# One fused two-block kernel: the context keys and values of the second block are computed at other places, gate products come in halves, and the expert rounds overlap

## The reference

```
first block:
  h = rmsnorm(x);  z = h @ w_in
  o_hg = gated recurrence over q, f_fw, f_bw, i (4 heads of 128, two directions), normed, gated
  o_mla = softmax attention, 8 heads of 96, keys and values from small latents
  merged = sigmoid(gate_a) * (o_hg @ w_oA) + sigmoid(gate_b) * (o_mla @ w_oB)
  x = x + merged @ w_out
  experts: hm = rmsnorm(x); top-1 of 8 groups, then top-2 of its 8 experts
           x += sum of weight * (silu(hm @ w1[e]) * (hm @ w3[e])) @ w2[e]
  x = x + (p @ w_ple_proj) * sigmoid(rmsnorm(x) @ w_ple_gate)
second block:
  hc = rmsnorm(ctx) * (1 + sc_c) + sh_c           # 256 context tokens
  k_c, v_c = split(hc @ w_in_2[:, K_OFF:V_END])   # two matrices of 1024 x 1024
  h = rmsnorm(x) * (1 + sc) + sh;  ten products h @ w_in_2[...]
  conv branch; 16-head neighbourhood attention over x's keys and k_c, v_c
  x = x + gt * rmsnorm(merged @ w_o)
```

## Time and profile before

| | us |
|---|---|
| median of 3 runs (1339.63 to 1343.4) | 1343.25 |
| the profiled execution | 1342.57 |
| its span, from first to last instruction | 1340.4 |
| TensorE busy in it | 1237.3 (92%) |
| VectorE, ScalarE, GpSimd busy | 302.1, 207.4, 107.1 |
| mean granted clock of TensorE | 0.959 of 2.4 GHz |
| moved by DMA | 324.57 MB |

### The profile page before, as it was taken

The page is one execution under the profiler, slowest core; times in us unless marked ns, Lnnn a source line. Parts: engine busy times, 40 slices in busy tenths (PEclk is TensorE's granted clock), DMA queues, the critical chain, the costliest instruction groups (busy, mean ns, idle before and its releaser), DMA issues.

```text
span 1340.4 us, 14669 instructions
## 1 busy us (share of the span) xinstructions
PE 1237.3 (92%) x6021; PEld 858.2 (64%) x6021; DVE 302.1 (23%) x652; ACT 207.4 (15%) x419; POOL 107.1 (8%) x117
## 2 busy tenths in 40 slices
PE   4999899999999989898989889889999999999997
PEld 4887788887853434434343324378888888876686
DVE  2035213543130111101110111121001004426511
ACT  1222452220110000000000000110000000025501
POOL 0015002510100000000000000000000000025300
PEclk9999899999989898898979898998999999999999
DMA  8879323333649999999999999952444444344300
GB/s 286 265 249 321 123 97 123 125 127 102 252 188 401 376 418 409 417 409 419 417 393 418 418 419 413 377 185 94 157 149 147 146 155 157 126 157 124 97 0 32
DMA packets 149737, 324.57 MB, mean 242 GB/s; under 512 B 8655, under 2 KB 111546, under 8 KB 133178
## 3 DMA queue, kind: packets, MB, share of 16 engines
q1 hardware_dynamic: 143818, 315.39, 63.0%
q0 software_dynamic: 1536, 4.20, 1.1%
q10 hardware_dynamic: 4336, 4.30, 1.0%
HBM read 321.77 MB, written 1.05 MB: 241 GB/s over the span
## 4 chain that ended last, share of the span: by engine, by line
PE 77%; DMA 8%; issue 7%; DVE 4%; ACT 2%; SPq 1%; POOL 1%; DVEq 0%; POOLq 0%; ACTq 0%
PE bank L551 31%; PE bank L817 14%; PE bank L554 13%; DMA ring<-in_w 7%; PE bank L837 5%; PE bank L794 3%; DVE X L1732 1%; PE bank L854 1%; PE bank L711 1%; PE bank L909 1%; DMA ring<-in_w_in 1%; PE bank L605 1%; PE bank L942 1%; PE bank L922 1%; ACT AR L1147 1%
## 5 line engine op out<-in xcount | busy, mean ns | idle before, releaser
L551 PE MATMUL bank<-HT,ring 128*128 128x256 f32 x1856 | 409.1, 382 | 4.3 <-DVE HT L1403 3.7
L551 PEld LDWEIGHTS bank<-HT,ring 128*128 128x128 f32 x1856 | 354.8, 192 | 56.4 <-DVE HT L1403 4.4
L817 PE MATMUL bank<-ring,AR 128*64 128x512 f32 x640 | 169.1, 593 | 3.9 <-DMA ring<-in_w 3.9
L554 PE MATMUL bank<-ring,HT 128*128 128x256 f32 (+1 forms) x576 | 129.1, 385 | 8.1 <-DMA ring<-in_w_in 6.9
L817 PEld LDWEIGHTS bank<-ring,AR 128*64 128x64 f32 x640 | 56.4, 137 | 112.9 <-issue 112.9
L554 PEld LDWEIGHTS bank<-ring,HT 128*128 128x128 f32 x576 | 110.3, 196 | 24.6 <-issue 8.2
L817 PE MATMUL bank<-AR 128*64 128x512 f32 x384 | 125.0, 663 | 0.1
L837 PE MATMUL bank<-ring,AR 128*64 128x512 f32 x384 | 87.7, 598 | 11.4 <-ACT AR L1147 11.4
L554 PE MATMUL bank<-ring,AR 128*128 128x256 f32 x328 | 74.5, 390 | 4.4 <-DVE AR L1850 1.5
L1720 DVE TENSOR_TENSOR AR<-AR,bank 128x256 f32<-128x256 f32 x32 | 13.5, 421 | 286.1 <-ACT AR L1140 286.1
L1267 POOL TENSOR_TENSOR SM<-SM 128x2 f32<-128x2 f32 (+3 forms) x9 | 12.3, 1368 | 787.7 <-DVE SM L1383 727.5
(11 more groups left out here) (307 smaller groups left out, 912.2 us busy)
## 6 DMA issues: line engine op xcount, KB each, us to landing
ring<-in_w SPq DMA_DIRECT2D x128, 1024.0 KB, 15.4
ring<-in_w_in SPq DMA_DIRECT2D x67, 1024.0 KB, 5.1
AR<-in_w SPq DMA_DIRECT2D x64, 1024.0 KB, 11.4
ring<-in_w_mod SPq DMA_DIRECT2D x12, 1024.0 KB, 6.0
ring<-in_w_out SPq DMA_DIRECT2D x4, 1024.0 KB, 6.0
ring<-in_w_ple_gate SPq DMA_DIRECT2D x4, 1024.0 KB, 9.7
ring<-in_w_out_conv SPq DMA_DIRECT2D x4, 1024.0 KB, 5.1
AR<-in_bias POOLq DMA_DIRECT2D x32, 128.0 KB, 2.4
```

What stands on the lines that cost most here:

```text
L551: mm = pe.matmul(bank[:, part * T:part * T + T], w[:, k, c0 + part * P:c0 + part * P + P], act[:, k, :], start=(k == 0), stop=(k == k_n - 1))
L554: mm = pe.matmul(bank[:, part * 256:part * 256 + n], act[:, k, part * P:part * P + P], w[:, k, c0:c0 + n], start=(k == 0), stop=(k == k_n ...
L817: mm = pe.matmul(bank[e * SLOT:e * SLOT + SLOT, :].rearrange("p (w n) -> p w n", w=2), XG[:, k, :], w, start=(k == 0), stop=(k == DK - 1))
```

## The change

- **Head.** X comes in two halves; the ring's loads follow at once on SyncE, and the eleven loads of small vectors are issued by ScalarE; ScalarE turns its half of x before it issues the other small loads. The angles of the rotary embedding come later on VectorE.
- **Gate products** come in halves (`gate_product`): one amid the turning of queries and keys, one ahead of the first scores, two in head 0, one in every other head, one ahead of levels 2 to 6. The last four gates are copied and get their sigmoid together. The running sums and the first levels move into the attention loop; each level's exponential is split in two, one for each operand.
- **Context** is turned in four pieces (`turn_context`) around the products `yb` and `ya`. Its eight products go: keys 0 around the logits, in two halves; three of keys and two of values into expert rounds 0, 1 and 2 (`context_product`, table `CTX_AT`), with loads of their own into the extra slots (`context_dma`); the last two of values behind the `ple` products. A third extra slot is added, and the first expert loads have another order. The copy of KC by a transfer falls away; logits and `ple` read tiles of their own (RHT, PLT).
- **Rounds** overlap: the next round's gather stands ahead of this round's last `up`, and the next round's first `up` ahead of the wait for X. Rounds 0 to 2 are written out.
- **Tail.** `wo` runs by halves of the tokens, with a norm and two stores for each.

```diff
-            sp.dma_start(X[:], a["x"][0].rearrange("(t p) d -> p t d", p=P)).then_inc(S("x_in"), 16)
+            for t in range(TT):
+                sp.dma_start(X[:, t, :], a["x"][0, t * P:t * P + P, :]).then_inc(S(f"x_in{t}"), 16)
...
-            sp.wait_ge(S("early_in"), EARLY)
...
+        CTX = [(wcols(w_in2, C_K + 256 * c, 256), "kc", c) for c in (1, 2, 3)] +\
+              [(wcols(w_in2, C_V + 256 * c, 256), "vc", c) for c in (0, 1)]
+        CTX_AT = {(0, 3): 0, (1, 1): 1, (1, 3): 2, (2, 1): 3, (2, 3): 4}
...
-        MRING, EXTRA = 12, (12, 13)
+        MRING, EXTRA = 12, (12, 13, 14)
...
-            for j in (4, 5, 6, 0, 1, 2, 3, 7, 8, 9, 10, 12, 13, 11):
+            for j in (4, 5, 0, 1, 2, 3, 12, 13, 14, 6, 7, 8, 9, 10, 11):
...
+            def context_dma(n):
+                if n < 2:
+                    sp.wait_ge(S("moe_used"), EXTRA[n] + 1)
+                else:
+                    sp.wait_ge(S("ctx_ps"), n - 1)
+                sp.dma_start(ctx_slot(n), CTX[n][0][0]).then_inc(S(f"arr_ctx{n % 2}"), 16)
+            ctx_behind = {(1, 1): 0, (1, 6): 1, (1, 14): 2, (2, 4): 3, (2, 14): 4}
+            for r in (1, 2):
+                g = sp.value_load(RT[0:1, r + 1:r + 2], min_val=0, max_val=NG - 1)
+                for j in range(NM):
+                    sp.wait_ge(S("moe_used"), r * NM + j - MRING + 1)
+                    expert_dma(j, g)
+                    if (r, j) in ctx_behind:
+                        context_dma(ctx_behind[(r, j)])
-            with sp.Fori(0, rounds - 1) as r:
+            with sp.Fori(2, rounds - 1) as r:
...
+            gate_halves = [(i, part) for i in of["gate"] for part in range(2)]
             for h in range(MH):
+                if h == 4:
+                    gate_product()
...
+            gate_product()
             mla_scores(0)
             for h in range(MH):
                 if h + 1 < MH:
                     mla_scores(h + 1)
+                if h == 0:
+                    gate_product()
                 mla_turn(h)
-                product(of["gate"][h], HT)
+                gate_product()
                 mla_values(h)
-            pe.wait_ge(S("normed"), nth("ctx", NORMED))
-            turn_rows(cols(HN))
-            pe.wait_ge(S("cT_dve"), 8)
-            context_product(4)
             for n, lv in enumerate(LEVELS):
-                context_product((0, 2, 2, 2, 2, 1, 1, 1)[n])
+                if 2 <= n < 7:
+                    gate_product()
                 pe.wait_ge(S("gla_qk"), n + 1)
...
+            product(of["kc"][0], HT, parts=(0,))
             pe.wait_ge(S("rT_dve"), 4)
...                                    (the logits, the turning of p)
+            product(of["kc"][0], HT, parts=(1,))
...
             def moe_round(r, first=False):
-                pe.wait_ge(S("sel"), at(1, 1))
-                if not first:
-                    pe.wait_ge(S("moe_x"), r)
-                ...                    (gather, sel_ps)
+                pe.wait_ge(S("gath"), at(1, 1))
                 up(0)
+                if not first:
+                    pe.wait_ge(S("moe_x"), r)
+                ...                    (STR and the weights of the lot)
                 for p in range(PAIRS):
+                    if p + 2 == PAIRS:
+                        pe.wait_ge(S("sel"), at(1, 2))
+                        gather()
                     if p + 1 < PAIRS:
                         up(p + 1)
                     turn_hidden(p)
                     down(p)
+                    if isinstance(r, int) and (r, p) in CTX_AT:
+                        context_product(CTX_AT[(r, p)], B[7 if p == 1 else 6])
...
             for i in of["ple"]:
-                product(i, HT, first=True)
+                product(i, PLT, first=True)
+            products("vc", HT)
...
-            products("wo", GA)
+            for t in range(TT):
+                for n, i in enumerate(of["wo"]):
+                    ...
+                    for k in range(DK):
+                        mm = pe.matmul(B[4 * t + n][:, 0:256], GA[:, k, t * P:t * P + P], slot_view(f)[:, k, :],
+                                       start=(k == 0), stop=(k == DK - 1))
```

More of the change, by code:

```diff
@@ L631, in _, with gate_product @@
             modulation_sum(pending)
+            gate_halves = [(i, part) for i in of["gate"] for part in range(2)]
+            def gate_product(n=1):
+                for _ in range(n):
+                    i, part = gate_halves.pop(0)
+                    product(i, HT, parts=(part,))
             pe.wait_ge(S("mod_in"), 1)
@@ L853, in moe_round @@
                         rows = slice(half * SLOT, half * SLOT + SLOT)
[L854 removed]
+                        mm = pe.matmul(B[SCATTER[2 * t + half]][:, :], STR[rows, t * P:t * P + P], YY[rows, :],
+                                       start=True, stop=True)
                 mm.then_inc(S("scat_ps"), 1)
@@ L859, in _ @@
             pe.wait_ge(S("normed"), nth("hm", NORMED))
-            moe_round(0, first=True)
+            pe.wait_ge(S("sel"), 1)
+            gather()
+            moe_round(FIRST, first=True)
+            for r in (1, 2):
+                moe_round(r)
+            pe.wait_ge(S("ctx_done"), len(CTX))
             pe.wait_ge(S("table"), 1)
             rounds = pe.value_load(RT[0:1, 0:1], min_val=4, max_val=ROUNDS)
-            with pe.Fori(1, rounds) as r:
+            with pe.Fori(3, rounds) as r:
                 moe_round(r)
@@ L1393, in normalize, with turned @@
                 ins.then_inc(S("normed"), 1)
-            def turned(tag, done, gain, ks=range(4), bias=None, first_bank=4):
+            def turned(tag, done, gain, ks=range(4), bias=None, first_bank=4, dst=HT):
                 for k in ks:
@@ L1736, in _ @@
             select()
-            moe_round(0)
+            dve.wait_ge(S("gath_ps"), 1)
+            gathered()
+            for r in range(3):
+                moe_round(r)
             rounds = dve.value_load(RT[0:1, 0:1], min_val=4, max_val=ROUNDS)
-            with dve.Fori(1, rounds) as r:
+            with dve.Fori(3, rounds) as r:
                 moe_round(r)
             mean_sq("ple", D)
-            turned("ple", "pleT_dve", lambda k: vec("ln_ple", k))
+            turned("ple", "pleT_dve", lambda k: vec("ln_ple", k), dst=PLT)
             for n, i in enumerate(of["ple"]):
@@ L1866 @@
+            for n in range(4):
+                out_gain(0, n)
+            out_norm(0)
+            out_gain(1, 0)
+            for half in range(2):
+                out_final(0, half)
+            for n in range(1, 4):
+                out_gain(1, n)
+            out_norm(1)
+            for half in range(2):
+                out_final(1, half)
 _NAMES = ["x", "p", "positions", "ln_mix", "w_in", "hg_lb", "hg_onorm", "w_oA", "mla_qa_norm", "mla_kva_norm", "w_uq",
```

437 lines of the change are left out of this document (256 added, 181 removed).

## The result

The changed kernel takes **1288.46 us** in the median of 4 runs (1285.28 to 1290.8), the kernel before 1341.44 in the same session (1334.73 to 1343.4). The ratio is 0.9616 with a 95% interval of 0.9589 to 0.9643: 3.8% faster. The forecast was 1286, its range 1270 to 1302. The profiled execution took 1288.38 us with a span of 1286.2, 54.2 less than the span before, where 56.5 were forecast.

A forecast was written before the change was run, and what follows sets the result against it. TensorE was taken as the limit ahead of and behind the experts, the DMA closely the limit in them. The terms -5.5 - 61.5 + 0 + 6.5 + 7 - 3 = -56.5 from 1342.6 gave 1286 us, range 1270 to 1302.

The forecast's parts named there:

- Head, -5.5: Kernel start: earlier loads and ScalarE turning its half at once start the first product at 15.5; bounds -3 and -6.6.
- Attention and recurrence, -61.5: First scores to recurrence's output products: eight context products and stalls leave, 65.8 us, against 4.5 us of level waits.
- lower bound (-50): Attention and recurrence: the gain is only 50 us if each level costs 1.5 more by GpSimd beside VectorE.
- rival C: Recurrence: GpSimd's subtractions stretch beside VectorE, each level takes 7 us, seven cost 12 more: 1298 us; chance 0.10.
- Outputs and routing, 0: Routing: one added context-key product, +6.9, is offset by a filled wait and faster clock; bounds -2 and +4.
- Experts, +6.5: Expert rounds: the DMA sets the end, five context loads add 16 us, stage 488.2 against 481.6; bounds -11 and +16.
- Rival A: Expert rounds become TensorE's if the clock falls in each: 498.5, ten more than the DMA's, 1297 us; chance 0.13.
- Behind the experts, +7: After the experts: two context value products, 13.8 us, partly fill TensorE's idle time; bounds +5 and +8.
- tail, -3: Kernel end: half the tokens' norm lies under matmuls, leaving an estimated 5.7 us instead of 8.5; bounds -2 and -4.
- D: Rival: the products were only cover, heads and levels keep their old pace, 9.1 and 8.7 us: 1348 us; chance 0.04.
- E: Rival: moved products cost all their time where they go, routing +4, experts +16, behind +8: 1301 us; chance 0.05.
- B: Rival for the expert rounds: a never-starved DMA runs 4% faster, TensorE's own sum of 470 decides: 1268 us; chance 0.08.

The follow-up runs named there:

- experiment 8: The changed kernel with ScalarE again issuing its twelve other small loads before turning its half of x, the ring's loads still early: 1299.39 us, ratio 0.9705.
- experiment 7: The changed kernel with SyncE again waiting for the small vectors' loads before it issues the ring's loads: 1289.25 us, ratio 0.9657.
- Experiment 5: The changed kernel with seven eighths of the contraction left out of the gate halves ahead of levels 2 to 6: 1289.59 us, stretch of levels 40.3 us against 40.2.
- experiment 6: The changed kernel with GpSimd's left-half subtractions of levels 2 to 4 replaced by zero fills: 1286.47 us, stretch of levels 36.2 us against 40.2.

## Why the prediction was right, and where not

*Head, -5.5 against -7.8.* The start at 15.5 was met (15.87, 5.1 earlier); the other 2.7 are the first 64 instructions, 11.49 us for 14.20, by experiment 8 the clock after an idle stretch, which I had not priced. The step that failed is the reason for the gain. I gave it to the ring's early issue; experiment 7 shows that this adds nothing where ScalarE turns first (56.80 and 57.00), experiment 8 that the order on ScalarE is worth 9.3 at the end of the stage. With the old order on ScalarE the early issue does not help either: experiment 8 ends the stage at 66.27, the kernel before, with late loads, at 64.78. Two things follow from that order. ScalarE turns its half of x late, which experiment 8 shows. And its loads' bytes run beside the ring's first load, which took 11.2 us before and at most 15.67 - 9.12 = 6.6 in experiment 7; that the bytes are the reason is argued from these two rows.

*Attention and recurrence, -61.5 against -59.0.* Heads as foretold. The mis-sized term is the levels' waits: spaced 5 to 5.24 us in the forecast, with 4.5 us of waits in all, the matmuls of levels 2 to 4 start 7 us apart (196.27, 203.24, 210.37), where both GpSimd and VectorE are at work: TensorE waits 2.60 and 1.73 us for VectorE, and 1.44 at the end. One level at a low clock (3.62 us for some 2.0) adds 1.6. Levels more than 6 us apart were one of my signs that the prediction is wrong; that much of it was, and it cost little because only these levels are so far apart. I had put it into the lower bound (-50) and into rival C, whose cause is thus real at a fifth of its price. Experiment 5 shows the chain, experiment 6 that GpSimd's part is in it. The Trainium skill ("SBUF — State Buffer", section "Who interferes with whom") has it that a VectorE operation with two inputs in SBUF contends with a GpSimd operation that reads SBUF, and that the lock on their shared ports is exclusive. An estimate by that rule is that VectorE's product ends its own 0.69 us behind the subtraction; in the trace it ends 0.55 us behind it both times, so the trace agrees to 0.14 us.

*Outputs and routing, 0 against -2.3:* within its bounds, at their lower end.

*Experts, +6.5 against +10.9.* Rounds 1 and 2 came out as forecast (67.4 and 66.4), the last four too (59.8), round 3 did not (53.2 for 60.2). The step that failed is that the DMA alone decides: without its five loads the products cost 15.8. That loads and products cost the same is luck, and it is why the sum came near. Rival A was wrong in its cause, for the granted clock is 1.00 in rounds 1 and 2, and right in that TensorE can decide. The 4.4 us over the forecast: the steady stream's first load is issued 333.71 - 314.33 = 19.4 us after the first gather, not 18.5 (0.9), the five loads cost 16.9, not 16 (0.9), and from 335 to 340 the DMA moves 374 GB/s while it starts (0.5). The forecast's term behind the last `up` holds: that product starts at 785.63, 21.2 us before the end. About 2 us stay open, less than two executions of one kernel differ by; without context work too the stage is 4.0 over the 472.2 that the forecast's terms give. That a wait in rounds 3 to 7 costs nothing while DMA is the limit was right: TensorE is not busy for 60 - 51.6 = 8.4 us of the third window above, and where an `up` is slow behind such a wait, as at 649.89, the DMA goes on at 419 GB/s (649 to 659). The last such slow `up` starts at 755.28 (8.78 us), and the next one, at 770.33, still waits 1.77 us for its transfer. The rule of the Trainium skill that the prediction weighed ("TensorE: Matmul & The Clock Gate", section "HAM oscillation — how this bites in real kernels") has the clock fall at such waits; the trace agrees in part: three `up`s behind waits of 3.47, 3.50 and 2.24 us take 8.8 us for 7.1, those behind 3.45 and 2.27 us take 7.1.

*Behind the experts, +7 against +7.0, and tail, -3 against -3.1 (second block included; 5.95 us behind the last gain, where 5.7 were estimated):* as worked out. Of the 7.0, 5.3 need not have been paid, as the values moved to X show: two products stand behind a wait that can hold one.

*Rivals.* D is ruled out by the heads' 5.65 us, E by the stages to which the products went: -2.3, +10.9 and +7.0 where it had +4, +16 and +8. B is out: the full DMA gave 417 to 418 GB/s, with and without context work.

*The sum.* 1286 for 1288.46 flatters the forecast. Its stages are off by -2.3, +2.5, -2.3 and +4.4 us, which make +2.3 together because they cancel.

## What to carry to other kernels

Where two resources are near a limit, a profile that shows one of them full says nothing about the other: take each one's extra work away alone, and then both, since here either cost 16 us and the second was free. When filler work is taken out from under a chain over several engines, price the chain with those engines beside each other, not by the rows in which they took turns. And before a gain is put down to one of two edits that come together, undo each: at the head of this kernel the one that looked like the cause gave nothing and its neighbour some 10 us.

## What was not expected of the hardware

- A small load's issue can hold the issuing engine for long: ScalarE's issue of 4 KB (LNM) took 4.59 us beside the ring's loads in experiment 8, 4.74 in the kernel before, and 6.62 us in the changed kernel, where nothing waits behind it; most others take 0.3 to 0.5.
- An idle stretch costs twice. In experiment 8, 7.93 us without work at the start were followed by a granted clock of 0.51 and 2.6 us more for the next 64 instructions; in the changed kernel the same instructions after an idle 0.98 us ran at 1.00.
- With 15 us of matmuls taken out from between the levels, the granted clock fell from 0.96 to 0.83 in the stretch, and two of the levels' own matmuls took 3.8 us; in the changed kernel one did (3.62), the others some 2.0.
- In the rounds that wait for transfers, an `up` took 8.8 us for 7.1 behind waits of 3.47, 3.50 and 2.24 us, but not behind 3.45 and 2.27. No time of the kernel hung on it, as the DMA stayed full.
